# Router logits straight in token rows, and the sums of squares in two products, in a two-layer hybrid transformer step

## The chip, the cores and the metric

The kernel runs on one core of a Trainium2 chip. The metric is the device time in microseconds (us) of one execution. A core has TensorE (PE in the profile; its weight loads are PEld), VectorE (DVE), ScalarE (ACT), GpSimd (POOL) and SyncE (SP, which issues most transfers), each with its own instruction stream; they meet at semaphores.

## The reference

One step of a model with two layers over 128 context rows and 256 sample rows, 384 tokens of 1024 features in float32. Per layer, cut to what matters here:

```python
h = rmsnorm(x, ln1_g) * (1 + sc1) + sh1           # norm 0
x = x + g1 * merge(conv(h), attention(h), mlstm(h), w_out)
h2 = rmsnorm(x, ln2_g) * (1 + sc2) + sh2          # norm 1
x = x + g2 * hier_moe(h2, w_rg, b_rg, w_re, b_re, w_gate, w_up, w_down)

def rmsnorm(x, g):
    return x * rsqrt(mean(x * x, axis=-1) + EPS) * g

def hier_moe(x, ...):
    gl = x @ w_rg + b_rg                          # 4 group logits
    el = (x @ w_re + b_re).reshape(N, 4, 4)       # 16 expert logits
    # best group, its two best experts, softmax weights; gated FFN of the chosen experts
```

After both layers comes one more rmsnorm with final_g. The router therefore needs 20 logits for each of the 384 tokens.

## The kernel before

Activations are kept transposed: features on the partitions in KT = 8 tiles of 128, the NT = 384 tokens in the free dimension (TILES = 3 blocks of 128). xT holds the residual, hT the normed input, mixT the mixer's output. Everything is unrolled by hand; each engine has its own stream, and PSUM is handed out in 8 banks by a planner, class Banks. place_products gives every product a bank; its helper spread deals names in turn over banks 0, 1, 2, 3, 4, 6, 7, and a product waits (wait_free) until the last user of its bank has been drained.

A norm goes in these steps. ScalarE squares the 8 tiles (L1264, into the buffer squares, which is hT). VectorE adds tile after tile into squares tile 0 (sum_square, L1515), 7 adds, each waiting for the last. TensorE multiplies that tile by a constant matrix of 1/1024 (sum_squares, L828), which gives the mean square of every token on all partitions. ScalarE takes the root (L1266), VectorE the reciprocal (L1522), then tile by tile the scaled input (L1526), and VectorE (L1529) and ScalarE (L1270) share the modulation. Norm 0 stands before the mixer, where the first product is gates (L840); norm 1 stands after w_out (L1015), whose residual adds (L1742) end one tile after the other, squares and adds following each. The final norm does the same with its own lines (L1451, L1932, L1225).

After norm 1 comes the router. Its product (L1045) has the 128x20 router weights of a feature tile as the stationary operand and the tile's 384 tokens moving, 8 calls into 20 partitions of one bank, named lgT. ScalarE copies it out (L1407), TensorE turns it by 3 transposes into bank lg (L1050), and VectorE adds the bias (L1756). A float32 product is two instructions with a weight load each; a transpose is one. TensorE goes on with 24 transposes of hT (h2, L1056), which ScalarE splits off as high parts (L1410) and VectorE as low parts (L1796, h2_rest: three before the selection matrices L1802, three after). Meanwhile VectorE finds group and experts (L1763 to L1783, ending in member). The rank products (L1064) wait for member; VectorE reads them at L1809 and copies them at L1812, and that copy frees the bank of rank. Then the 8 gathers gA (L1080, banks 6, 7, 0, 1, 4, 5, 2, 3) bring the tokens of each expert together, and the expert stage runs in 8 pairs (L1123, L1164, L1104), followed by a loop for overflow jobs, whose gather is L1080 with 64 columns. SyncE streams the expert weights into 10 slots; a transfer into a slot waits for TensorE's last read of it (wait_chunk_read).

Of the kernel before, what the change touches and what calls it, by code (L numbers as in the profile page):

```python
# [34 lines left out]
P = 128  # L35
# [157 lines left out]
def place_products(bk, layer):  # L193

    turn = [0]

    def spread(*names, over=(0, 1, 2, 3, 4, 6, 7)):
        for name in names:
            bk.place(name, over[turn[0] % len(over)])
            turn[0] += 1  # L200

    def mod(which, c):

        if c % 4 == 0:
            bk.place(("mod", which, c // 4), 5)
        if c % 4 == 3:
            bk.place(("modT", which, c // 4), 5)

    if layer == 0:
        spread(("vec", 0), ("vec", 1))  # L210
        for c in range(4):
            mod(0, c)
    spread(("ss", 0))
    before_heads = (0, 1, 2, 3, 4)
    for kind, *args in mixing_steps(layer):
        if kind == "gates":
            spread("gates")
        elif kind == "by_token":
            spread(tuple(args), over=before_heads)
        elif kind == "by_feature":  # L220
            spread(("fm", *args), over=before_heads)
        elif kind == "mod":
            mod(*args)
        elif kind == "gate_columns":
            spread("rowsA", "rowsB", over=before_heads)
        elif kind == "old_keys":
            spread("old_keys", over=before_heads)
        elif kind == "turn":
            spread(("turn", *args), over=before_heads)
        elif kind == "context_scores":  # L230
            spread(("sp", 0), ("sp", 1), over=before_heads)
        elif kind == "scores":
            spread(("scores", *args), over=before_heads)
        elif kind == "context_turn":
            spread("pTc", over=before_heads)
        elif kind == "turn_probs":
            spread(("pT", *args), over=before_heads)
        elif kind == "context_values":
            bk.place(("o", 0), 6)
            bk.place(("o", 1), 7)  # L240
        elif kind == "decay":
            spread(("mu", *args), ("kq", *args), ("int", *args))
        elif kind == "read":
            spread(("num", *args), ("C", *args))
    spread(*[("wo", m) for m in range(EARLY_OUT)], *[("hT", h) for h in range(4)],
           *[("wo", m) for m in range(EARLY_OUT, 8)], ("ss", 1))
    spread("lgT", "lg", *[("h2", i) for i in range(6)], "rank")
    for k in range(8):
        bk.place(("gA", k), (6, 7, 0, 1, 4, 5, 2, 3)[k])
    for j in range(PAIRS):  # L250
        bk.place(("G", j), 2)
        bk.place(("U", j), 3)
        if j > 0:
            for m in range(8):
                bk.place(("back", j - 1, m), 6 + m % 2)
        bk.place(("selT", j), 0)
        bk.place(("gs", j), 4)
        for x in range(4) if j in GATHER_AFTER else ():
            bk.place(("gB", GATHER_AFTER.index(j), x), 6 + x % 2)
        bk.place(("aT", j), 1)  # L260
        bk.place(("y", j, 0), 4)
        bk.place(("y", j, 1), 5)
    for m in range(8):
        bk.place(("back", PAIRS - 1, m), 6 + m % 2)
    bk.in_job = True
    for name, bank in (("lxg", 0), ("lgu", 2), ("lselT", 1), ("laT", 3), ("ly", 4)):
        bk.place(name, bank)
    for n, m in enumerate(BACK_ORDER):
        bk.place(("lback", m), (5, 6, 7, 0)[n % 4])
    bk.in_job = False  # L270
# [163 lines left out]
def build(nc, a, o):  # L434
    D, FF, NT, TILES, DEPTH = 1024, 512, 384, 3, 2
    KT = D // P
# [4 lines left out]
    with ExitStack() as ctx:  # L441
# [15 lines left out]
        hT = sb("hT", [P, KT, NT])  # L457
        mixT = sb("mixT", [P, KT, NT])
# [3 lines left out]
        arena = sb("arena", [P, 6668])  # L462
# [22 lines left out]
        wroute = sb("wroute", [P, KT, 20])  # L485
# [15 lines left out]
        ident = cst[:, C_IDENT:C_IDENT + P]  # L501
        ones = cst[:, C_ONES:C_ONES + P]
        mean = cst[:, C_MEAN:C_MEAN + P]
# [22 lines left out]
        loop_selT = hidden[:, 2560:2944]  # L526
        loop_selw = arena[:, 4480:4864].rearrange("p (t n) -> p t n", t=3)
        loop_tmp = arena[:, 4864:5632].rearrange("p (b t n) -> p b t n", b=2, t=3)
        lgT = arena[0:20, 0:NT]
        squares = hT  # L530

        xrow = ring[:, RING - 1, 0:3072].rearrange("p (t d) -> p t d", t=3)
# [39 lines left out]
        def scratch(n, pattern=None, **sizes):  # L572
# [15 lines left out]
        ps = [ctx.enter_context(nc.psum_tensor(f"ps{b}", [P, 512], F32)) for b in range(BANKS)]  # L588
# [6 lines left out]
        fin_sq, fin_summed, fin_sum, fin_root, fin_scaled = (  # L595
            sem(n) for n in ("fin_sq", "fin_summed", "fin_sum", "fin_root", "fin_scaled"))
# [189 lines left out]
        def _(pe):  # L786
            pe.wait_ge(const_loaded, 16)
            pe.wait_ge(x_loaded, 32)
            for k in range(KT):
                for t in range(TILES):  # L790
                    mm = pe.transpose(ps[k][:, t * P:(t + 1) * P], xrow[:, t, k * P:(k + 1) * P], ident)
                mm.then_inc(x_turned, 1)

            for ly in layers:
                bk = ly.bk

                def begin(name, job=None):
                    bk.wait_free(pe, name, job)
                    return ps[bk.bank(name)]

                def done(mm, name):
                    mm.then_inc(bk.full[bk.bank(name)], 1)
# [21 lines left out]

                def sum_squares(n):
                    p = begin(("ss", n))
                    pe.wait_ge(ly.summed_ready, (n + 1) * (KT - 1))
                    done(pe.matmul(p[:, 0:NT], mean, squares[:, 0, :], start=True, stop=True), ("ss", n))  # L828

                def wait_normed(n, k):  # L830

# [158 lines left out]
                if ly.first:  # L990
                    pe.wait_ge(vecs_loaded, 16 * 9)
                    pe.wait_ge(x_copied, KT)
                    for d in range(DEPTH):
                        p = begin(("vec", d))
                        n = V_ROWS if d == 0 else V_C
# [30 lines left out]
                for h in range(4):  # L1026
                    pe.wait_ge(ly.hnorm_ready, h + 1)
                    p = begin(("hT", h))
                    for t in range(TILES):
                        mm = pe.transpose(p[:, t * P:(t + 1) * P], hsum[:, t, h * P:(h + 1) * P], ident)  # L1030
# [8 lines left out]
                sum_squares(1)  # L1039


                p = begin("lgT")
                for k in range(KT):
                    wait_normed(1, k)
                    mm = pe.matmul(p[0:20, 0:NT], wroute[:, k, :], hT[:, k, :], start=(k == 0), stop=(k == KT - 1))  # L1045
                done(mm, "lgT")
                bk.wait_drained(pe, "lgT")
                p = begin("lg")
                for t in range(TILES):
                    mm = pe.transpose(p[:, t * 20:(t + 1) * 20], lgT[:, t * P:(t + 1) * P], ident[0:20, 0:20])  # L1050
                done(mm, "lg")
                for i in range(6):
                    upper, t = i // 3, i % 3
                    p = begin(("h2", i))
                    for n in range(4):
                        mm = pe.transpose(p[:, n * P:(n + 1) * P], hT[:, upper * 4 + n, t * P:(t + 1) * P], ident)  # L1056
# [3 lines left out]
                p = begin("rank")  # L1060
# [24 lines left out]
                for k in range(KT):  # L1085
# [3 lines left out]
                    p = begin(("gA", k))  # L1089
# [18 lines left out]
                for j in range(PAIRS):  # L1108
# [7 lines left out]
                    for k in range(KT):  # L1116
# [4 lines left out]
                        for i in range(4):  # L1121
                            which, s = "GGUU"[i], i % 2
                            mm = pe.matmul(out[which][64 * s:64 * s + 64, :], xg[:, k, cols[s]], w[i][:, k % 4, :],  # L1123
                                           start=(k == 0), stop=(k == KT - 1))
# [9 lines left out]
                    p = begin(("selT", j))  # L1134
                    for t in range(TILES):
                        mm = pe.transpose(p[:, t * P:(t + 1) * P], sel[:, t, pair_cols], ident)
                    done(mm, ("selT", j))
                    p = begin(("gs", j))
                    if j == 0:
                        pe.wait_ge(ly.jobs_ready, ly.number + 1)  # L1140
                    for t in range(TILES):
                        mm = pe.matmul(p[:, 0:32], sel_r[:, t, pair_cols], gates_split[:, t, :],
                                       start=(t == 0), stop=(t == 2))
# [77 lines left out]
                                       start=True, stop=True), ("lback", m))  # L1221


            pe.wait_ge(fin_summed, KT - 1)
            pe.matmul(ps[0][:, 0:NT], mean, mixT[:, 0, :], start=True, stop=True).then_inc(fin_sum, 1)  # L1225
            for i in range(6):
                pe.wait_ge(fin_scaled, 4 * (i % 2) + 4)
                for n in range(4):
# [5 lines left out]
        def _(act):  # L1234
# [14 lines left out]
            for ly in layers:  # L1249
                bk, L = ly.bk, ly.number  # L1250

                def drain(name, ins):
                    ins.then_inc(bk.drained[bk.bank(name)], 1)

                def full_of(name, job=None):
                    bk.wait_full(act, name, job)
                    return ps[bk.bank(name)]
# [145 lines left out]
                    drain(("hT", h), act.copy(mixT[:, 4 + h, :], p[:, 0:NT]))  # L1403
                norm(1)

                p = full_of("lgT")
                drain("lgT", act.copy(lgT, p[0:20, 0:NT]))  # L1407
                for i in range(6):
                    p = full_of(("h2", i))
                    act.copy(h2_high[:, i % 3, (i // 3) * 512:(i // 3 + 1) * 512], p[:, :]).then_inc(ly.h2_high_ready, 1)  # L1410
# [48 lines left out]
        def _(dve):  # L1459
# [17 lines left out]
            for ly in layers:  # L1477
# [29 lines left out]

                def sum_square(n, k):

                    if k == 0:  # L1510
                        return
                    dve.wait_ge(ly.squares_ready, n * KT + k + 1)
                    if k > 1:
                        dve.wait_ge(ly.summed_ready, n * (KT - 1) + k - 1)
                    dve.tensor_tensor(squares[:, 0, :], squares[:, 0, :], squares[:, k, :], ALU.add  # L1515
                                      ).then_inc(ly.summed_ready, 1)

# [407 lines left out]
                        bk.wait_drained(dve, ("lback", m), job)  # L1925
                dve.sem_inc(ly.x_done, 1)

            for k in range(1, KT):
                dve.wait_ge(fin_sq, k + 1)
                if k > 1:  # L1930
                    dve.wait_ge(fin_summed, k - 1)
                dve.tensor_tensor(mixT[:, 0, :], mixT[:, 0, :], mixT[:, k, :], ALU.add).then_inc(fin_summed, 1)  # L1932
# [33 lines left out]
```

## Time and profile before

| | |
|---|---|
| median of 3 runs | 1345.16 us (1340.98 to 1346.26) |
| profiled execution | 1342.49 us, span 1339.6 us |
| PE busy | 1177.6 us, 88% of the span, 6150 instructions |
| DVE busy | 426.9 us, 32% |
| ACT busy | 248.4 us, 19% |
| chain that ended last | PE 74%, DMA 12%, DVE 9%, ACT 3% |
| mean granted TensorE clock | 0.94 |

A time in a row is in us from the start of the span. A matmul's duration reaches from its start to its modelled end, so back-to-back matmuls overlap in the rows; their pace is read from start to start. The granted clock is given as a share of 2.4 GHz.

### The profile page before, as it was taken

To read this page: it belongs to the slowest core of one execution; us is meant where nothing else is said; L and a number is where in the kernel's file an instruction comes from. 1 tells how busy PE (TensorE), PEld (TensorE's weight loads), DVE (VectorE), ACT (ScalarE), POOL (GpSimd) and SP (SyncE) were. 2 spreads that over 40 slices of the span, in tenths; PEclk is the share of its full clock that TensorE was granted. 3 is DMA by queue.
4 is the path that set the end of the run, shared out by engine and by line. 5 is a ranking of instruction groups with operands and counts; after the bars stand their busy time and mean duration, and the time that the engine had idled before them with its cause. 6 is when DMAs were issued, how large, how long until landed. Compare 5 with 4: busy or idle time off the path is not lost.

```text
span 1339.6 us, 15169 instructions
## 1 busy us (share of the span) xinstructions
PE 1177.6 (88%) x6150; PEld 630.2 (47%) x6150; DVE 426.9 (32%) x1183; ACT 248.4 (19%) x511; POOL 41.2 (3%) x64
## 2 busy tenths in 40 slices
PE   3699989899778999999859998989977999999884
PEld 3346545576453343433524554557635334343352
DVE  2502031346441323233261203135544132322325
ACT  1210121232231011110032012114222101111012
POOL 1500000000020000000000000000000000000000
PEclk9799989899889999999679997999988999999967
DMA  9936333484319999999351453234430999999911
GB/s 350 312 108 243 142 126 126 160 312 111 125 38 403 414 402 396 403 399 413 144 189 63 173 212 126 72 119 156 113 124 1 403 413 399 401 392 407 410 62 47
DMA packets 95365, 315.10 MB, mean 235 GB/s; under 512 B 5964, under 2 KB 6208, under 8 KB 86464
## 3 DMA queue, kind: packets, MB, share of 16 engines
q1 hardware_dynamic: 91712, 306.43, 59.9%
q0 software_dynamic: 3584, 7.71, 2.2%
q8 instruction: 49, 0.80, 0.2%
q14 instruction: 20, 0.16, 0.0%
HBM read 310.92 MB, written 4.99 MB: 236 GB/s over the span
## 4 chain that ended last, share of the span: by engine, by line
PE 74%; DMA 12%; DVE 9%; ACT 3%; issue 2%; SPq 1%; DVEq 0%; ACTq 0%
PE ps L850 15%; PE ps L1123 12%; DMA ring<-in_w_up 10%; PE ps L860 8%; PE ps L1164 6%; PE ps L1080 5%; PE ps L1015 5%; PE ps L812 3%; PE ps L1104 3%; PE ps L1190 1%; PE ps L1105 1%; PE ps L967 1%; DMA ring<-in_w_mod 1%; PE ps L840 1%; PE ps L1045 1%
## 5 line engine op out<-in xcount | busy, mean ns | idle before, releaser
L1123 PE MATMUL ps<-ring,arena 128*64 128x512 f32 x832 | 241.2, 601 | 18.6 <-DMA ring<-in_w_up 18.5
L850 PE MATMUL ps<-ring,hT 128*128 128x512 f32 (+1 forms) x480 | 198.2, 572 | 0.0
L1742 DVE SCALAR_TENSOR_TENSOR xT<-ps,modT,xT 128x128 f32<-128x128 f32 x320 | 115.8, 411 | 237.0 <-PE ps L1105 175.0
L850 PEld LDWEIGHTS ps<-ring,hT 128*128 128x128 f32 x480 | 91.8, 193 | 100.2 <-issue 97.1
L1164 PE MATMUL ps<-ring,arena 128*64 128x512 f32 x384 | 115.0, 605 | 8.1 <-ACT arena L1430 8.1
L1123 PEld LDWEIGHTS ps<-ring,arena 128*64 128x64 f32 x832 | 66.7, 136 | 114.0 <-issue 114.0
L860 PE MATMUL ps<-hT,ring 128*128 128x384 f32 x320 | 106.2, 489 | 0.0
L1123 PE MATMUL ps<-slot,arena 128*64 128x512 f32 x192 | 94.5, 600 | 1.4 <-issue 1.4
L1015 PE MATMUL ps<-mixT,ring 128*128 128x384 f32 x256 | 83.4, 487 | 1.5 <-ACT mixT L1403 1.5
L860 PEld LDWEIGHTS ps<-hT,ring 128*128 128x128 f32 x320 | 59.8, 190 | 40.7 <-issue 0.8
L1902 DVE SCALAR_TENSOR_TENSOR y_low<-ps,route,y_high 128x512 fp32r<-128x512 f32 x32 | 24.0, 751 | 136.6 <-ACT y_high L1434 135.9
L1104 PEld LDWEIGHTS ps<-selT,y_high 128*128 128x128 f32 x128 | 24.7, 193 | 90.2 <-issue 79.5
L1015 PEld LDWEIGHTS ps<-mixT,ring 128*128 128x128 f32 x256 | 48.3, 190 | 34.8 <-issue 1.9
L1164 PEld LDWEIGHTS ps<-ring,arena 128*64 128x64 f32 x384 | 34.9, 139 | 59.6 <-issue 49.2
L1104 PE MATMUL ps<-selT,y_high 128*128 128x384 f32 x128 | 57.0, 445 | 4.6 <-DVE y_low L1902 3.4
L1164 PE MATMUL ps<-slot,arena 128*64 128x512 f32 x128 | 57.3, 595 | 2.7 <-ACT arena L1430 2.7
L812 PE MATMUL ps<-ring,csil 128*32 128x128 f32 x1536 | 52.0, 293 | 8.2 <-DMA ring<-in_w_mod 6.1
L1420 ACT ACTIVATE arena<-ps 128x512 f32<-128x512 f32 x16 | 9.6, 597 | 250.3 <-PE ps L1123 250.3
L1496 DVE COPY modrow<-ps 128x512 f32<-128x512 f32 x6 | 4.1, 692 | 158.8 <-PE ps L812 158.8
L812 PEld LDWEIGHTS ps<-ring,csil 128*32 128x32 f32 x1536 | 45.1, 118 | 16.2 <-DMA ring<-in_w_mod 6.6
L1080 PE MATMUL ps<-sel_r,h_high 128*128 128x256 f32 (+1 forms) x144 | 44.8, 338 | 8.0 <-DVE h_low L1796 7.8
L1105 PE MATMUL ps<-selT,y_low 128*128 128x384 f32 x128 | 45.0, 352 | 0.0
(308 smaller groups left out, 1300.5 us busy)
## 6 DMA issues: line engine op xcount, KB each, us to landing
ring<-in_w_up SPq DMA_DIRECT2D x56, 1024.0 KB, 10.4
ring<-in_w_gate SPq DMA_DIRECT2D x54, 1024.0 KB, 13.9
ring<-in_w_down SPq DMA_DIRECT2D x50, 1024.0 KB, 9.9
ring<-in_w_mod SPq DMA_DIRECT2D x24, 2048.0 KB, 12.5
ring<-in_w_in SPq DMA_DIRECT2D x14, 2048.0 KB, 9.1
slot<-in_w_down SPq DMA_DIRECT2D x18, 1024.0 KB, 12.0
slot<-in_w_gate SPq DMA_DIRECT2D x14, 1024.0 KB, 12.9
slot<-in_w_up SPq DMA_DIRECT2D x12, 1024.0 KB, 9.7
```

Of the source, the lines that this page charges most:

```text
L812: mm = pe.matmul(p[32 * g:32 * g + 32, (c % 4) * P:(c % 4 + 1) * P], csil[:, k, :], w[:, k, g * P:(g + 1) * P], start=(k == 0), stop=(k == ...
L840: mm = pe.matmul(p[:, 0:NT], wgp[:, k, :], hT[:, k, :], start=(k == 0), stop=(k == KT - 1))
L850: mm = pe.matmul(p[:, 0:n], hT[:, k, t * P:(t + 1) * P], w[:, k, c0:c0 + n], start=(k == 0), stop=(k == KT - 1))
L860: mm = pe.matmul(p[:, 0:NT], w[:, k, (i % 4) * P:(i % 4 + 1) * P], hT[:, k, :], start=(k == 0), stop=(k == KT - 1))
L1015: mm = pe.matmul(ps[bk.bank(("wo", m))][:, 0:NT], w[:, k, (m % 4) * P:(m % 4 + 1) * P], mixT[:, k, :], start=(k == 0), stop=(k == KT - 1))
L1080: mm = pe.matmul(out, part[:, t, interleaved(k, FEATURE_RUN)], selected[t], start=(t == 0 and part is h2_high), stop=(t == 2 and part is h ...
L1104: pe.matmul(p[:, 0:NT], y_high[:, m * P:(m + 1) * P], selT[:], start=True, stop=False)
L1105: done(pe.matmul(p[:, 0:NT], y_low[:, m * P:(m + 1) * P], selT[:], start=False, stop=True), ("back", j, m))
L1123: mm = pe.matmul(out[which][64 * s:64 * s + 64, :], xg[:, k, cols[s]], w[i][:, k % 4, :], start=(k == 0), stop=(k == KT - 1))
L1164: mm = pe.matmul(out[y][64 * s:64 * s + 64, :], aT[:, f * P + 64 * s:f * P + 64 * s + 64], w[s][:, f % 2, y * 512:(y + 1) * 512], start=(f ...
L1742: ins = dve.scalar_tensor_tensor(xT[:, m, cols], p[:, cols], modT[:, L, gate0 + m, j:j + 1], xT[:, m, cols], ALU.mult, ALU.add)
L1902: drain(("y", j, y), dve.scalar_tensor_tensor(y_low[:, of_half], p[:, :], gate_slot, y_high[:, of_half].bitcast(F32), ALU.mult, ALU.subtract))
```

## The change

Two things. The router product swaps its operands: a 128x128 block of hT (features by tokens) is stationary and the 128x20 router weights move, so the logits come out with tokens on the partitions, three blocks side by side in one bank. The bank lgT, the copy and the three transposes go. And VectorE no longer adds the last squared tile: TensorE multiplies the sum of tiles 0 to 6 as soon as it is there, and the last tile in a second product into the same bank.

```diff
-    spread("lgT", "lg", *[("h2", i) for i in range(6)], "rank")
+    spread("lg", *[("h2", i) for i in range(6)], "rank")
...
                 def sum_squares(n):
                     p = begin(("ss", n))
-                    pe.wait_ge(ly.summed_ready, (n + 1) * (KT - 1))
-                    done(pe.matmul(p[:, 0:NT], mean, squares[:, 0, :], start=True, stop=True), ("ss", n))
+                    pe.wait_ge(ly.summed_ready, (n + 1) * (KT - 2))
+                    pe.matmul(p[:, 0:NT], mean, squares[:, 0, :], start=True, stop=False)
+                    pe.wait_ge(ly.squares_ready, (n + 1) * KT)
+                    done(pe.matmul(p[:, 0:NT], mean, squares[:, KT - 1, :], start=False, stop=True), ("ss", n))
...
-                p = begin("lgT")
+                p = begin("lg")
                 for k in range(KT):
                     wait_normed(1, k)
-                    mm = pe.matmul(p[0:20, 0:NT], wroute[:, k, :], hT[:, k, :], start=(k == 0), stop=(k == KT - 1))
-                done(mm, "lgT")
-                bk.wait_drained(pe, "lgT")
-                p = begin("lg")
-                for t in range(TILES):
-                    mm = pe.transpose(p[:, t * 20:(t + 1) * 20], lgT[:, t * P:(t + 1) * P], ident[0:20, 0:20])
+                    for t in range(TILES):
+                        mm = pe.matmul(p[:, t * 20:(t + 1) * 20], hT[:, k, t * P:(t + 1) * P], wroute[:, k, :],
+                                       start=(k == t == 0), stop=(k == KT - 1), skip_group_check=True)
                 done(mm, "lg")
...
-            pe.wait_ge(fin_summed, KT - 1)
-            pe.matmul(ps[0][:, 0:NT], mean, mixT[:, 0, :], start=True, stop=True).then_inc(fin_sum, 1)
+            pe.wait_ge(fin_summed, KT - 2)
+            pe.matmul(ps[0][:, 0:NT], mean, mixT[:, 0, :], start=True, stop=False)
+            pe.wait_ge(fin_sq, KT)
+            pe.matmul(ps[0][:, 0:NT], mean, mixT[:, KT - 1, :], start=False, stop=True).then_inc(fin_sum, 1)
...
-                p = full_of("lgT")
-                drain("lgT", act.copy(lgT, p[0:20, 0:NT]))
...
                 def sum_square(n, k):
 
-                    if k == 0:
+                    if k == 0 or k == KT - 1:
                         return
                     dve.wait_ge(ly.squares_ready, n * KT + k + 1)
                     if k > 1:
-                        dve.wait_ge(ly.summed_ready, n * (KT - 1) + k - 1)
+                        dve.wait_ge(ly.summed_ready, n * (KT - 2) + k - 1)
...
-            for k in range(1, KT):
+            for k in range(1, KT - 1):
```

## Rows read from the trace of the kernel before

**Rows 1.** Chain of waits, layer 0: start us, us, what.

```profile
358.62 1.12 PE ps L828 x2
364.65 7.67 PE ps L1045 x16
...
372.34 0.48 ACT arena L1407
...
383.50 12.79 PE ps L1080 x48
...
418.43 14.19 DMA ring<-in_w_up
```

**Rows 2.** Timeline of layer 0: start us, us, engine, line, what.

```profile
368.20 0.73 DVE L1529 TENSOR_SCALAR hT<-hT,gains,modT 128x256 f32<-128x256 f32 x2
...
373.15 2.84 PE L1056 MATMUL ps<-cst,hT 128*128 128x128 f32 x24
373.26 0.22 DVE L1756 TENSOR_TENSOR arena<-ps,rbias 128x60 f32<-128x60 f32 x1 [4.33 <-PE ps L1050]
...
378.29 1.55 PE L1064 MATMUL ps<-arena,cst 128*128 128x16 f32 x12 [2.30 <-DVE arena L1783]
...
380.62 0.20 DVE L1809 TENSOR_TENSOR route<-ps,arena 128x48 f32<-128x48 f32 x1
...
382.67 1.88 DVE L1796 TENSOR_TENSOR h_low<-ps,h_high 128x512 fp32r<-128x512 f32 x3
```

**Rows 3.** Timeline of layer 1, the same columns.

```profile
998.20 6.62 PE L1045 MATMUL ps<-hT,wroute 128*20 128x384 f32 x16 [4.93 <-DVE hT L1529]
...
1001.75 0.73 DVE L1529 TENSOR_SCALAR hT<-hT,gains,modT 128x256 f32<-128x256 f32 x2
...
1005.77 0.22 DVE L1756 TENSOR_TENSOR arena<-ps,rbias 128x60 f32<-128x60 f32 x1 [3.30 <-PE ps L1050]
...
1010.80 2.51 PE L1064 MATMUL ps<-arena,cst 128*128 128x16 f32 x12 [2.30 <-DVE arena L1783]
...
1013.35 0.21 DVE L1809 TENSOR_TENSOR route<-ps,arena 128x48 f32<-128x48 f32 x1
...
1015.41 1.88 DVE L1796 TENSOR_TENSOR h_low<-ps,h_high 128x512 fp32r<-128x512 f32 x3
1017.21 0.21 DVE L1812 COPY arena<-ps 128x64 f32<-128x64 f32 x1
...
1017.43 0.77 PE L1080 MATMUL ps<-sel_r,h_high 128*128 128x512 f32 x1 [4.12 <-DVE h_low L1796]
```

**Rows 4.** TensorE by stretches: us, PE busy (x), granted clock, DMA share, GB/s.

```profile
646.60:656.60 10.00, 10.00 (x47) 0.50 0.18 66
364.60:369.10 4.50, 4.45 (x8) 0.50 0.00 0
369.20:372.30 3.10, 3.10 (x10) 0.97 0.00 0
998.20:1000.90 2.70, 2.70 (x5) 0.51 0.00 0
...
17.80:18.70 0.90, 0.32 (x2) 1.00 1.05 385
...
991.70:993.30 1.60, 0.88 (x2) 1.00 0.76 282
1321.90:1324.20 2.30, 1.65 (x2) 0.50 0.00 0
```

**Rows 5.** The overflow job's gathers in layer 0: duration ns min/median/max, first and last start.

```profile
L1080 PEld LDWEIGHTS ps<-loop_sel,h_high x24: 288/331/332, 646.6 to 656.3; 128*128 128x128 f32 x24
...
L1080 PE MATMUL ps<-loop_sel,h_low x24: 401/401/402, 646.8 to 656.6; 128*128 128x64 f32 x24
```

**Rows 6.** Timeline: the first transposes, and the adds of the first norm.

```profile
12.28 5.35 PE L791 MATMUL ps<-cst,ring 128*128 128x128 f32 x24 [12.28 <-DMA ring<-in_x_sample]
...
39.63 4.47 DVE L1515 TENSOR_TENSOR hT<-hT 128x384 f32<-128x384 f32 x7
```

More of the change, by code:

```diff
@@ L528, in build @@
         loop_tmp = arena[:, 4864:5632].rearrange("p (b t n) -> p b t n", b=2, t=3)
-        lgT = arena[0:20, 0:NT]
         squares = hT
```

## The prediction

> **What bounds the kernel now.** I read the chain of waits first. The page gives TensorE 74% of it and DMA 12%. In the stretch the change touches the chain is a serial relay, one piece at a time with nothing beside it: product for the sum of squares (L828), root, reciprocal, scaled tiles, router product (L1045), a ScalarE copy (L1407), three transposes (L1050), the logits on VectorE, and later the first gather (L1080) [rows 1]. So here every microsecond counts in full. What follows cannot give it back: the expert stage is paced in turns by TensorE and by the w_up transfers, and a transfer into a slot is issued only when TensorE has read the slot's last content (wait_chunk_read), so a late gather moves the transfers by as much. That long DMA piece stands in [rows 1].
>
> Then the timelines of the two layers. Router product to logits takes 373.26 - 364.65 = 8.6 us in layer 0 [rows 1, 2] and 1005.77 - 998.20 = 7.6 us in layer 1 [rows 3]. The work is the same; the difference is the granted clock. TensorE had been nearly idle while the norm was made, and the product starts at 0.50 (1.2 GHz) in both layers. It climbs to 2.4 GHz at 369.1 in layer 0 and at 1000.9 in layer 1 [rows 4]. A call is two instructions, 0.64 us apart at the low clock and 0.32 at the full one (8 in 4.5 us, 10 in 3.1 us) [rows 4]. The last scaled tile is there at 368.20 + 0.73 = 368.9 and 1001.75 + 0.73 = 1002.5 [rows 2, 3], before TensorE's last calls: TensorE, not the norm, ends this wait.
>
> **The router product.** Removed per layer: 8 calls of 384 moving columns, the copy (0.48 us) and its two hand-overs, 3 small transposes. Added: 24 calls, 48 instructions, each with a 128x128 weight load and 20 moving columns. The nearest rows are the rank products (L1064: 128x128 f32 weights, 16 to 48 columns) and the gathers of the overflow job (L1080, 64 columns). Twelve rank instructions take 1.55 us in layer 0 at the full clock [rows 2]: less a last one of 0.30, 0.11 us each. The overflow gathers go from 646.8 to 656.6 in 46 steps: 0.213 us each [rows 5], at the low clock [rows 4]. 20 columns are fewer than both, so the load sets the pace: 0.11 or 0.213.
>
> Which clock? The overflow gathers ran 10 us without a gap, TensorE 10.00 of 10.00 us busy, and the grant stayed at 0.50 all the time [rows 4]. They keep the array as the new product would: long load, few columns. The old 384-column product climbed after 2.7 to 4.4 us. I therefore take the low clock for all 48: 47 x 0.2135 + 0.37 for the last one + 0.04 to VectorE = 10.45 us from the first product to the logits. Against 8.6 that is +1.85 in layer 0, against 7.57 it is +2.9 in layer 1: +4.75 us. Bounds: 48 at 0.11 from the point where the old product climbed (a rival below), and 48 unoverlapped loads of 0.331 us [rows 5], 15.9 us.
>
> Here a rule of the Trainium skill speaks. TensorE: Matmul & The Clock Gate, section LDWEIGHTS (loading the stationary operand), says that a load costs its columns divided by 1.2, in ns, however few rows or bytes: some 107 ns for 128 columns. By it 48 loads are an estimated 5.1 us whatever the clock. The trace agrees at the full clock (0.11) and not at the low one (0.213). The same rule also speaks against the change: swapping operands turns 20-column loads into 128-column ones.
>
> **What stands behind it.** The h2 transposes (24, L1056) now start at the low clock too: 24 initial transposes took 5.35 us there [rows 6], against 2.84 [rows 2]. That puts their end about 15.5 us after the product began; the member mask on VectorE is ready 5.04 us after the logits (378.29 - 373.26 [rows 2]), 10.45 + 5.04 = 15.5 as well. So they are just hidden, with no slack. The rank products after them: logits-side L1809 starts 2.33 us after them in layer 0 and 2.55 in layer 1 (mixed clock) [rows 2, 3]; wholly at the low clock 11 x 0.213 + 0.37 + 0.04 = 2.75. That is +0.4 and +0.2, or nothing if the transposes lift the clock. I take +0.2 in sum.
>
> **Banks.** Dropping "lgT" moves every later name of that spread one place. Counting the placement through: bank 6, which gA 0 takes, was h2 3 in layer 0 and h2 5 in layer 1; it becomes h2 4 and "lg" then "rank". TensorE's first gather starts 0.15 us after VectorE drains that bank's last user: 383.50 in layer 0, while h2 3 to 5 are drained from 382.67 on, 0.60 us apart [rows 1, 2]; 1017.43 in layer 1, after the third of them (1015.41 + 1.88) [rows 3]. New: one drain later in layer 0, +0.60; in layer 1 after the rank copy L1812 (1017.21 + 0.21) instead, +0.13. Sum +0.73. The other banks of the gathers come free before their turn, 48 instructions taking 12.79 us for eight gathers [rows 1]. ScalarE, rid of its copy, waits longer for h2 and gains nothing.
>
> **The sum of squares, five times.** VectorE's adds follow each other every (4.47 - 0.56)/6 = 0.65 us [rows 6], so the product can start 0.65 us sooner, and it has two instructions more. In the three where TensorE has idled long (both first norms, the final one) the grant is 0.50 and the pair takes 1.65 us (the final one stands for the three [rows 4]). Two more at 0.64 are +1.28, less 0.65: +0.62 each, +1.85 in all. In the second norms TensorE has just finished w_out. In layer 1 the grant is 1.00 and the pair takes 0.88 [rows 4]; two more at 0.32 are +0.65: nothing. In layer 0 the clock falls in the middle (1.12 us [rows 1]); starting earlier gets more of it done at full clock, -0.15. Sum +1.7. Bounds: 0 if all ran at the full clock, +3.1 if all ran at the low one. The last square on ScalarE is long there when it is needed, so the new wait on it costs nothing; behind that wait stands only the product itself. VectorE's spared add covers nothing else: it waits for the root.
>
> **Sum.** 4.75 + 0.2 + 0.73 + 1.7 = +7.4 us. The profiled execution took 1342.49 us (span 1339.6), so 1349.9 for such a one. The median of three is 1345.16, and 1342.49 lies inside their spread (1340.98 to 1346.26); the mean of the four is 1343.7. On these the sum gives 1351.1 to 1352.5; I say 1352.
>
> **Rivals.**
> Clock climbs (chance 0.10; not slower): the grant rises during the new product where it did during the old one. Layer 0: 21 instructions in the first 4.4 us, 27 at 0.11, logits after 7.75 us, -0.85; layer 1: 13 in 2.8 us, 35 at 0.11, 7.0 us, -0.55. With banks and squares +1.0: 1346. It decides from the rise onward. For it: after the 5.35 us of transposes (L791) the next two products (L996) ran at the full clock [rows 4, 6]. Against it: the ten microseconds of gathers.
> Loads at 0.11 at either clock (0.04; about the same): TensorE then follows the scaled tiles, ends 1.0 us after the last one: 370.0 and 1003.5, -3.3 and -2.3; with the rest -3.2: 1342. This is what the skill's load rule would make of it.
> The delay hides in the transfers (0.06): if the expert stage's transfers were running ahead, only the squares would count, +1.7: 1347. Against it the issue rule above.
> Loads don't overlap (0.04): 15.9 us per product, +11 more: 1363. Against it the 0.213 steps between loads of 0.331 [rows 5].
> The forecast (0.76): 1352, its own range 1349 to 1355. A gain above 0.5% needs several of the small terms to be wrong at once.
>
> **Numbers.** 0.5% of 1345 is 6.7 us, about what a measurement of this kernel can tell from no change, and the forecast of 7.4 stands right at it. Just over half of its 0.76 falls beyond: 0.42, with the unoverlapped loads 0.46 slower. The rest of it and the three cases around no change give 0.50, faster 0.04. Range: from the climbing clock at 1346 to 1357, the upper end being the squares' bound (+1.4 over what I took), +0.4 from the rank products and some 3 us, half of the spread of the runs shown.
>
> **What would show it.** The new product's 48 instructions 0.213 us apart at granted clock 0.50, 10 us long, logits some 10.5 us after its start; the first gather at 0.15 us after the drain of h2 4 in layer 0 and after L1812 in layer 1; first norms and final norm with four instructions in some 2.9 us. Wrong if the grant rises inside the product, or if the ends of the sums of squares don't move later.

## The result, and the profile after

In 20 runs each the changed kernel took 1347.09 us in the median, the kernel before 1339.72; the ratio is 1.0053, 95% interval 1.0036 to 1.0070: slower by 7.1 us (4.8 to 9.4). The changed kernel's median lies inside the range of 1346 to 1357 and below the forecast's own 1349 to 1355. The runs of before that the prediction had, 1345.16 in the median, lay high. The profiled execution took longer by more than that, span 1349.9 us against 1339.6; where the rest of the 10.3 us comes from stands further down. Of all executions on record two had a lower mean granted clock than the rest, 1788.04 us at 0.647 (e8 below) and 1457.37 us at 0.814 (e4); the ratios leave them out, the medians don't.

The chain of waits of the changed kernel in layer 0, against [rows 1]:

```profile
358.56 0.88 PE ps L827 x2
...
359.44 0.66 PE ps L829 x2
...
365.01 10.41 PE ps L1047 x48
...
375.45 0.23 DVE arena L1754
...
386.30 14.03 PE ps L1078 x48
```

The copy and the transposes are gone, and the product that replaced three steps takes longer than the three did: 375.45 - 365.01 = 10.44 us from its start to the logits, before 8.6. The last row is the eight first gathers: they start 2.80 us later and then also take 14.03 us where they took 12.79, a part of the loss that the prediction doesn't have; it is taken up below. Both layers' timelines, against [rows 2] and [rows 3]:

```profile
375.25 4.32 PE L1054 MATMUL ps<-cst,hT 128*128 128x128 f32 x24
...
380.49 1.51 PE L1062 MATMUL ps<-arena,cst 128*128 128x16 f32 x12 [0.93 <-DVE arena L1781]
...
382.83 0.20 DVE L1807 TENSOR_TENSOR route<-ps,arena 128x48 f32<-128x48 f32 x1
...
384.87 1.88 DVE L1794 TENSOR_TENSOR h_low<-ps,h_high 128x512 fp32r<-128x512 f32 x3
...
386.30 0.77 PE L1078 MATMUL ps<-sel_r,h_high 128*128 128x512 f32 x1 [4.29 <-DVE h_low L1794]
```

```profile
1004.80 10.40 PE L1047 MATMUL ps<-wroute,hT 128*128 128x20 f32 x48 [4.93 <-DVE hT L1527]
...
1015.24 0.22 DVE L1754 TENSOR_TENSOR arena<-ps,rbias 128x60 f32<-128x60 f32 x1 [6.16 <-PE ps L1047]
...
1020.28 1.42 PEld L1062 LDWEIGHTS ps<-arena,cst 128*128 128x128 f32 x12 [0.29 <-DVE arena L1781]
...
1024.66 1.88 DVE L1794 TENSOR_TENSOR h_low<-ps,h_high 128x512 fp32r<-128x512 f32 x3
1026.45 0.21 DVE L1810 COPY arena<-ps 128x64 f32<-128x64 f32 x1
1026.81 0.76 PE L1078 MATMUL ps<-sel_r,h_high 128*128 128x512 f32 x1 [5.02 <-DVE arena L1810]
```

Layer 1 shows the same 10.44 us (before 7.6), although the two layers differed before. The last row shows the bank at work: the first gather waits for L1810, the copy of the ranks, where before it waited for the low parts (L1796 in [rows 3]). In layer 0 it starts 1.43 us after 384.87, before 0.83 after 382.67.

TensorE by stretches (columns as in [rows 4]) says why the two layers agree:

```profile
365.10:375.20 10.10, 10.10 (x48) 0.50 0.01 2
375.30:378.30 3.00, 3.00 (x16) 0.50 0.00 0
378.40:380.40 2.00, 1.17 (x11) 1.00 0.00 0
380.50:381.90 1.40, 1.40 (x12) 1.00 0.00 0
1004.90:1015.00 10.10, 10.10 (x48) 0.50 0.01 2
...
43.80:46.60 2.80, 2.80 (x4) 0.50 1.04 334
998.40:999.80 1.40, 1.40 (x4) 1.00 0.76 281
```

TensorE was busy without a gap for 10 us and the grant stayed at 1.2 GHz. The transposes behind it began at the low clock and ended at the full one. The fifth row is the router of layer 1. The last two are sums of squares, now four instructions each: the first norm of layer 0 lies at the low clock and takes 2.93 us from its first start to its last end, the second norm of layer 1 at the full one and takes 1.53.

### The profile page after: what moved, and what is told of

The parts are those of the page before. It is cut to its first block, busy times and chain, and to the rows that moved or that the text cites. A ratio compares the mean times of both kernels' runs of the same rounds, so it can differ in the third digit from the quotient of the medians.

```text
span 1349.9 us, 15292 instructions
## 1 busy us (share of the span) xinstructions
PE 1194.8 (89%) x6218; PEld 653.3 (48%) x6218; DVE 423.7 (31%) x1178; ACT 248.1 (18%) x509; POOL 41.1 (3%) x64
## 4 chain that ended last, share of the span: by engine, by line
PE 76%; DMA 10%; DVE 9%; ACT 2%; issue 2%; SPq 0%; DVEq 0%; ACTq 0%
PE ps L851 15%; PE ps L1121 14%; DMA ring<-in_w_up 8%; PE ps L861 8%; PE ps L1162 6%; PE ps L1078 5%; PE ps L1016 5%; PE ps L811 3%; PE ps L1102 3%; PE ps L1047 2%; PE ps L968 1%; PE ps L1103 1%; PE ps L1188 1%; DMA ring<-in_w_mod 1%; PE ps L841 1%
## 5 line engine op out<-in xcount | busy, mean ns | idle before, releaser
L1078 PE MATMUL ps<-sel_r,h_low 128*128 128x256 f32 (+1 forms) x144 | 44.5, 337 | 0.0
```

The source lines that it names most:

```text
L1078: mm = pe.matmul(out, part[:, t, interleaved(k, FEATURE_RUN)], selected[t], start=(t == 0 and part is h2_high), stop=(t == 2 and part is h ...
```

## The experiments

Times are medians beside runs of the kernel before on the same chip; local steps are read from each kernel's trace, of which there is one for each kernel.

**Either part alone (e1, e2).** One kernel has only the router's part of the diff, the other only that of the squares.

> Only the router product in token rows, the sums of squares as before. If the router carries most of the loss: logits 10.45 us after the product's start in both layers (before 8.6 and 7.6), first gather +0.60 and +0.13 us later against its drains, sum about +5.6 us against before. If the loss sat in the sums of squares instead (rival): within 2 us of before.

> Only the sums of squares in two products, the router as before. Theory: the root starts 0.62 us later in the two first norms and the final one (granted clock 0.50), about 0.2 us earlier or the same in the two second norms (clock 1.00); +1.5 us in sum, hardly to be told from no change by time. Rival (the spared add pays off): root 0.65 us earlier everywhere, -3 us.

The router alone: 1347.75 us, ratio 1.0061 (1.0038 to 1.0084), which is 8.2 us (5.1 to 11.3) where about 5.6 were expected. Product to logits 10.44 us in both layers, first gather 1.43 and 2.16 us after the second group of low parts begins. So the router carries most of the loss, and its rival falls. The squares alone: 1345.05 us, ratio 1.0037 (1.0018 to 1.0057), clearly not a gain. From the start of ScalarE's last square to the start of the reciprocal, read in the traces:

| norm | before | changed | squares only |
|---|---|---|---|
| first norm, layer 1 | 4.95 us | 5.57 | 5.57 |
| final norm | 4.95 us | 5.56 | 5.57 |
| second norm, layer 0 | 3.21 us | 2.95 | 2.95 |
| second norm, layer 1 | 2.99 us | 2.95 | 2.95 |

+0.62 twice, and a third time in the first norm of layer 0 (first add to reciprocal 6.82, changed 7.44); -0.26 and -0.04 in the second norms: +1.6 us in sum, where +1.5 was expected. The timed difference of 0.37% is 5 us, its lower end 2.4. These local steps don't account for that, and the two parts' ratios add up to more than the whole's; the difference between kernels timed in 12 and 6 runs stays open. In the profile of e2 (span 1344.9 us, 5.3 more than before) 3.2 us arise in layer 1's mixer, at a lower grant, which is taken up at the end; whether they do in its other executions isn't on record.

**The bank (e3).** One line puts every later name back in its old bank.

```diff
+    turn[0] += 1
     spread("lg", *[("h2", i) for i in range(6)], "rank")
```

> The changed kernel, but the spread skips one turn where lgT stood, so that every later name has the bank it had before. Theory: the first gather starts 0.83 us after the second group of low parts begins in layer 0 (changed kernel 1.43) and 2.02 us in layer 1 (changed kernel 2.15), 0.73 us less in all. If the banks don't release it (rival): 1.43 and 2.15 stay.

Timeline of this kernel, layer 0:

```profile
386.16 1.88 DVE L1795 TENSOR_TENSOR h_low<-ps,h_high 128x512 fp32r<-128x512 f32 x3
386.99 0.77 PE L1079 MATMUL ps<-sel_r,h_high 128*128 128x512 f32 x1 [3.70 <-DVE h_low L1795]
```

0.83 us in layer 0 again, and 2.03 in layer 1: both as before, 0.72 us less than the changed kernel. The time, 1345.2 us and ratio 1.0045 (1.0019 to 1.0071), is too coarse for it. That the bank's last user releases the first gather is shown by the trace.

**More moving columns over the same loads (e5 with 40, e4 with 120).** Every router call moves the 20 weights several times over, twice in e5 and six times in e4; only the first copy is read. The 48 loads of 128x128 stay. The edit of e4:

```diff
-                        mm = pe.matmul(p[:, t * 20:(t + 1) * 20], hT[:, k, t * P:(t + 1) * P], wroute[:, k, :],
+                        mm = pe.matmul(p[:, t * 120:(t + 1) * 120].rearrange("p (c n) -> p c n", c=6),
+                                       hT[:, k, t * P:(t + 1) * P],
+                                       wroute[:, k, None, :].broadcast_to((P, 6, 20)),
                                        start=(k == t == 0), stop=(k == KT - 1), skip_group_check=True)
```

> The changed kernel with every router call's moving columns doubled to 40 (the 20 weights twice; the second copy isn't read), same 48 weight loads. If the weight load sets the pace: 0.213 us from start to start at granted clock 0.50 as with 20 columns, logits still 10.4 us after the start. If columns or their writes count (rival): slower per instruction, over 11 us.

> The changed kernel with 120 moving columns in every router call (the 20 weights six times; only the first copy is read), the same 48 loads of 128x128. If the low granted clock is what makes the product long and few moving columns are what leaves it low: the grant rises inside the product, the later instructions come 0.11 us apart, logits 7 to 8.7 us after the start although six times the columns are moved, and about 4 us less than the changed kernel. If the swap is slow for another reason (rival): 10.4 us or more, time no better than the changed kernel.

With 40 columns the logits come 10.47 us after the start in both layers (10.44 with 20), at 0.50 throughout; the kernel ran once, 1347.56 us. With 120, layer 0 (timeline, then TensorE by stretches):

```profile
363.77 7.08 PE L1047 MATMUL ps<-wroute,hT 128*128 128x120 f32 x48 [4.93 <-DVE hT L1529]
...
370.69 2.78 PE L1056 MATMUL ps<-cst,hT 128*128 128x128 f32 x24
370.89 0.22 DVE L1756 TENSOR_TENSOR arena<-ps,rbias 128x60 f32<-128x60 f32 x1 [2.83 <-PE ps L1047]
```

```profile
363.80:366.80 3.00, 3.00 (x14) 0.50 0.00 0
367.00:370.30 3.30, 3.30 (x32) 1.00 0.02 5
```

Six times the columns, and 3.3 us less: logits 7.12 us after the start in layer 0 and 8.01 in layer 1 (changed kernel 10.44 in both). The grant rose after 3 us in layer 0 (in layer 1 only after some 4.8, at 1005.0), and from there on twice as many instructions fit into the same time. So the 24 calls and their 48 loads don't make the product this long by themselves; the 1.2 GHz it stays at does. In time: 1341.77 us, ratio 1.0031 (1.0007 to 1.0055), which lies below the changed kernel's but overlaps it.

**TensorE kept busy while it waits (e6).** Calls on constants into a bank that nobody uses at the time; nothing reads their results.

```diff
+            def warm(bank, calls):
+                for _ in range(calls):
+                    pe.matmul(ps[bank][:, 0:NT], mean, cst[:, 0:NT], start=True, stop=True)
...
+                bk.wait_free(pe, ("gA", 5))
+                warm(5, 1)
                 sum_squares(1)
+                warm(5, 6)
```

> The changed kernel with idle TensorE filled around the second norm: one 384-column call into an unused bank ahead of the sum of squares and six after it, results unread. Theory: the router product starts at granted clock 1.00, then 0.11 us per instruction, TensorE follows the scaled tiles, logits about 5.3 us after the first product (changed kernel 10.4); some 10 us less than the changed kernel, 3 less than before. Rival (24 swapped calls are slow at any clock, or the fillers run into the product): logits 8 us or more after the start.

Missed. Layer 0, timeline and stretches:

```profile
359.62 4.03 PE L791 MATMUL ps<-cst 128*128 128x384 f32 x12
...
364.71 9.06 PE L1054 MATMUL ps<-wroute,hT 128*128 128x20 f32 x48 [1.06 <-DVE hT L1534]
```

```profile
364.70:366.10 1.40, 1.39 (x13) 1.00 0.00 0
366.30:373.50 7.20, 7.20 (x36) 0.50 0.01 2
```

The product did start at the full clock, and after 1.4 us the grant fell in the middle of it, with TensorE busy all the time. Logits 9.10 us after the start, 8.11 in layer 1, where 5.3 were expected. So the 20-column product not only went through at the low clock, it also lost the full one that it was given. That this goes with its columns, and not with the 1.06 us of waiting before it, is shown by e7 against e9 below: the same fillers and the same 1.06 us, 20 and 120 columns, and only the first loses the clock. The overflow job's gathers (64 columns over 128x128 loads) do the same without any filler. Changed kernel, layer 0, start and rest of the gathers from 650.9 us on:

```profile
650.90:651.30 0.40, 0.40 (x4) 1.00 1.02 374
651.60:660.40 8.80, 8.80 (x43) 0.50 0.03 13
```

The kernels of this case other than e8 have 24 such runs of 48 gathers in their profiles. Ten began at 0.50 and none of them rose; fourteen began at 1.00 and all of them fell, one as late as some 4 us after its start (e4, layer 1). The time, 1341.08 us, ratio 1.0017 (0.9999 to 1.0036), is no gain over before.

**The same everywhere, with the new (e7) and the old router (e8).** Fillers also in the first norms (5 or 8 calls ahead of the sum, 6 after), before the rank products (2), before the first gather (4) and in the final norm (8 and 7).

> As the filled router, with the banks kept and fillers also in the first norms, before the rank products, before the first gather and in the final norm. Theory: router as there; sums of squares in the first norms and the final one at granted clock 1.00, root no later than before; gates product 5.3 us and not 7.5; first gathers at the full clock (3 to 4 us less at the low clock per layer). In sum 12 to 18 us less than before. Rival (fillers delay the real work, or the clock falls all the same): no better than before by more than 5 us.

> The kernel before (old router product, one product for the squares) with the same fillers. Theory: it gains the same from the clock but keeps the copy and the three transposes, logits about 6.3 us after the product's start, so some 2 us slower than the filled kernel with token rows. Rival (the swap is worse even at the full clock): faster than that one.

New router: 1332.43 us, ratio 0.9959 (0.9940 to 0.9978), by the ratio 5.5 us less than before and not the 12 to 18 expected; logits 7.42 and 8.14 us after the start, the clock falling inside again. The eight first gathers took 11.4 us in each layer, 1.4 and 1.8 less than before, where 3 to 4 were expected. Old router: 1330.74 us, ratio 0.9933 (0.9910 to 0.9956). The kernel that loses the swap is at least as fast, against my theory that token rows would win at a kept clock. Its profile tells nothing of the steps, so the same kernel ran again (e10), beside the version that follows from all this, fillers everywhere and 120 columns (e9), and that one with the old squares (e11).

> The same kernel as e8_old_filled_all, for a profile at an undisturbed clock. Theory: the 384-column product holds the clock it starts at, 0.32 us per instruction, logits 6.2 to 6.4 us after its start in both layers; sum of squares pair 0.88 us in all five norms. Some 1 us per layer slower than e9_filled_wide. Rival (the copy and the transposes cost less than the swap's loads): as fast as e9_filled_wide or faster.

> Fillers everywhere (as in e7_filled_all) and 120 moving columns in every router call (as in e4_wide120), the six-fold weights read once. Theory: the product now both starts at granted clock 1.00 and holds it, 0.11 us per instruction, TensorE follows the scaled tiles, logits about 5.3 us after the first product (e7_filled_all 7.4 and 8.1); about 5 us less than e7_filled_all, so some 12 us less than before. Rival (the clock falls inside the product also with 120 columns): 7 us or more after the start, no better than e7_filled_all.

> e9_filled_wide with the old sums of squares (seven adds, one product). Theory: at the full clock an add (0.65 us) and a two-instruction product (0.65 us) cost the same, so the roots start within 0.1 us of e9_filled_wide after the squares, and the times agree within noise. Rival (the second product is what costs, at any clock): about 3 us faster than e9_filled_wide.

Layer 0 of e9, then of e10 (timelines), and the stretch of each one's router product:

```profile
362.60 5.67 PE L1057 MATMUL ps<-wroute,hT 128*128 128x120 f32 x48 [1.06 <-DVE hT L1543]
...
368.31 0.22 DVE L1770 TENSOR_TENSOR arena<-ps,rbias 128x60 f32<-128x60 f32 x1 [1.43 <-PE ps L1057]
```

```profile
361.06 5.55 PE L1054 MATMUL ps<-hT,wroute 128*20 128x384 f32 x16 [1.06 <-DVE hT L1542]
366.65 0.47 ACT L1420 COPY arena<-ps 20x384 f32<-20x384 f32 x1 [1.43 <-PE ps L1054]
...
367.57 0.22 DVE L1769 TENSOR_TENSOR arena<-ps,rbias 128x60 f32<-128x60 f32 x1 [2.23 <-PE ps L1059]
```

```profile
362.60:368.20 5.60, 5.60 (x49) 1.00 0.01 3
```

```profile
361.10:366.60 5.50, 5.50 (x16) 1.00 0.01 3
```

| | product to logits, layer 0, 1 | median | ratio to before |
|---|---|---|---|
| e9: fillers, 120 columns | 5.71, 5.71 us | 1326.45 us | 0.9910 (0.9887 to 0.9933) |
| e10: fillers, old router | 6.51, 6.51 us | 1328.70 us | 0.9931 (0.9907 to 0.9954) |
| e11: as e9, old squares | 5.71, 5.71 us | 1325.51 us | 0.9912 (0.9880 to 0.9944) |

At a clock that holds, the two products take nearly the same (5.67 and 5.55 us), and what token rows save is the copy and the transposes: 0.8 us per layer, seen in the trace and too small for the timed ratios. Two products for the squares against seven adds: 4.20 and 4.21 us from the start of the last square to the reciprocal in layer 1's first norm. A draw, as expected. The product of e9 missed its 5.3 us by 0.4: its 48 instructions, 0.12 us apart, set the pace, and not the scaled tiles it follows. e10's 6.5 us lie just over the 6.2 to 6.4 expected; its two-instruction sums of squares take 0.88 to 0.91 us in all five norms, as expected. e9 is 12 us faster than the kernel before (9 to 15). Most of that comes from the fillers and not from the swap: e10 has the old router and is 9.2 us faster. Which of the fillers pay was not tried one by one.

## Why the prediction was right

**The clock and the load's pace.** Both held: 10.44 us in each layer where 10.45 was worked out. The term was +4.75, measured (10.44 - 8.60) + (10.44 - 7.58) = +4.7. The old product's share of it moves with the moment at which the clock rises: in e2 it took 7.86 and 8.74 us, which would make the term +4.3. That the moving columns don't set the pace at the low clock is shown by 20 and 40 columns taking the same time; that the clock makes the rest, by 120 columns taking less. That it is the load, and not a fixed cost of each instruction, no run tests with this product. It agrees with L812, whose loads have 32 columns and which turns through four groups of partitions: at a grant of 0.50 (22.0 to 24.0 us, kernel before) its instructions came about 0.05 us apart. The unoverlapped loads and the loads at 0.11 us at either clock, the one by the skill's rule, are both out. By that rule (Trainium skill, TensorE: Matmul & The Clock Gate, LDWEIGHTS) 48 loads were an estimated 5.1 us; the product took 10.4 us at the low clock, and 5.7 only at the full one (e9, with 120 columns).

**The climbing clock** was the rival nearest to the truth about its mechanism: it happens, with 120 columns and not with 20 or 40. The evidence that the prediction gave for it doesn't hold, though. It took the first 24 transposes (L791, 5.35 us) for low-clock ones after which the grant rose for L996. But the grant reads 1.00 from the start of the span to beyond L996, the transposes included, so these rows show no rise. The price was right all the same: in layer 1 of the changed kernel the 24 transposes took 5.26 us, at 0.50 up to 1019.0.

**What stands behind.** The transposes began at the low clock and were hidden, as forecast, and with little slack: TensorE idled 0.93 us in layer 0 and 0.29 in layer 1 between them and L1062, which waited for the member mask on VectorE. The clock rose while they ran, in time for the ranks in both layers, so L1807 begins 2.34 us after L1062 in both; against 2.33 and 2.55 before the term is -0.2 where +0.2 was forecast.

**Banks.** +0.60 and +0.13 forecast, 1.43 - 0.83 = 0.60 and 2.15 - 2.02 = 0.13 measured, and taken back by one line in e3.

**Squares.** +0.62 each at the low clock, measured 0.62 three times; -0.15 and 0 in the second norms, measured -0.26 and -0.04. Sum +1.6 for +1.7.

**The sum.** By local steps 4.7 - 0.2 + 0.73 + 1.6 = 6.8 us, by time 7.1 (4.8 to 9.4). That these agree so well is partly luck: the interval is 4.6 us wide, e2's timed 5 us stay unexplained, and the sum leaves out what the clock did behind the router. In layer 0 the eight first gathers took 1.24 us longer, because the grant rose 5.7 us after their start (at 392.0) where it had risen after 2.9 (at 386.4); in layer 1 they took 0.17 us less. So the expert stage begins 4.05 us late in layer 0 (397.00 and 401.05) and 9.20 in layer 1 (1031.36 and 1040.56).

"What follows cannot give it back" holds in layer 1, where the stage also ends 9.27 us late. In layer 0 the difference moves between 3.0 and 6.0 us along the stage, and 2.99 are left at its end, so 1.06 us came back. The last 0.8 of that came in the overflow job's products right behind its gathers (L1190, L1188 in the changed kernel), where the grant rose sooner; what part the transfers had in the rest was not tried. The rival that hides the whole delay in the transfers falls in any case. The level was off by more than the difference: I took 1345.16 for the kernel before, and 20 runs give 1339.72.

**The profile's other 3.5 us.** Some 3.0 of them arise in layer 1's mixer, which the change doesn't touch: from the reciprocal of its first norm to the first square of its second, 270.79 us before and 273.81 after. Another 0.4 arises behind the last reciprocal. TensorE from 900 to 920 us, before and after:

```profile
900.00:920.00 20.00, 17.52 (x155) 0.91 0.90 345
```

```profile
900.00:920.00 20.00, 15.27 (x111) 0.66 0.98 367
```

The grant was low there for longer in one execution than in the other. Over the same 20 us the grant was 0.91 in e1, e3, e5 and e6, where that part of the mixer took 270.1 to 270.4 us, and 0.66 or 0.67 in e2 and e4, where it took 273.9 and 273.8. Kernels with the new router stand on both sides, and so do kernels with the new squares, so it goes with neither part of the change. Whether it goes with anything else in the kernels, or only with the execution, was not tried: each kernel has one profile.

## What to carry to other kernels

Swapping a product's operands so that few columns move over full loads saves the turn behind it, but where TensorE comes out of a wait, ask first at which granted clock it will start and whether the new product will let it rise: the old product's length hid a rise that the new one never got. Moving the same weights several times over, with the copies unread, can be the cheaper call: 7.12 and 8.01 us for 10.44 here. An unused wait of TensorE on a serial path can be worth filling, and more so with a product that then keeps the clock: 0.9959 with 20 columns behind the fillers (e7), 0.9910 with 120 (e9), in different sets of runs.
When a name is dropped from a list that hands out banks in turn, count through who gets which bank before whom; here that cost 0.7 us in a place far from the edit.

## What the runs showed of the hardware that I had not expected

The grant fell inside a gapless product: 48 instructions of 20 columns over 128x128 loads started at 1.00 and were at 0.50 after 1.4 us in layer 0 and some 2.6 in layer 1 (e6). The overflow job's gathers, with 64 columns, never raised the grant and always lost it. With 120 columns over the same loads it rose from 0.50 in 3 us (e4) and held at 1.00 (e9). For the router product nothing between 40 and 120 columns was tried.
An instruction with 128x128 float32 weights came every 0.213 us at 1.2 GHz with 20, 40 and 64 moving columns.
